# Down products two steps behind the up products in a float32-precise decoder trunk, with every hidden tile turned by DMA and the bias bands loaded in fewer transfers

## The reference

```python
def swiglu(x, w_gate_up, w_down):
    gate, up = jnp.split(x @ w_gate_up, 2, axis=-1)      # 1024 x 5632
    return (jax.nn.silu(gate) * up) @ w_down             # 2816 x 1024

for layer in range(2):
    h = mixer_a(...) if layer == 0 else mixer_b(..., rel_bias)
    x = x + rms_norm(h @ w_o, g[1])
    h = swiglu(rms_norm(x, g[2]), w_gate_up[layer], w_down[layer])
    x = x + rms_norm(h, g[3])

bias = rel_bias[relative_bucket(rel * dilation)]         # a function of the distance, one per head
s = (q @ k) * scale + bias, masked; softmax; @ v
```

## Time and profile before

| | us |
|---|---|
| three runs, median (range) | 759.71 (758.87 to 760.59) |
| profiled execution | 757.09 |
| its span, first to last instruction | 755.3 |
| outside the span | 1.8 |
| PE busy | 744.8 (99%) |
| DVE busy | 531.9 (70%) |
| ACT busy | 416.7 (55%) |
| POOL busy | 175.4 (23%) |

### The profile page before, as it was taken

One profiled execution on the slowest core, in us unless ns is written; L12 is line 12 of the kernel. 1 busy time (PEld: TensorE's weight loads), 2 busy tenths in 40 slices (PEclk: granted clock), 3 DMA queues, 4 the chain that ended last, 5 costly groups with the idle time before them and its releaser, 6 DMA issues.

```text
span 755.3 us, 13376 instructions
## 1 busy us (share of the span) xinstructions
PE 744.8 (99%) x4616; PEld 639.5 (85%) x4616; DVE 531.9 (70%) x766; ACT 416.7 (55%) x619; POOL 175.4 (23%) x298
## 2 busy tenths in 40 slices
PE   9999999999999999999999999999999999999996
PEld 7999987888888888999898898898878888888884
DVE  5888997776766657777777677677557675666653
ACT  4766667444343344865855867766576434433421
POOL 1000001225100000146664664666502000000000
PEclk9999999999999999999999999999999999999999
DMA  8645585699976675559798897897743797767602
GB/s 251 198 126 162 181 245 186 187 275 231 239 250 202 184 223 136 164 157 242 182 219 175 207 190 194 190 223 210 242 140 98 252 277 217 213 192 233 228 14 56
DMA packets 190756, 147.16 MB, mean 195 GB/s; under 512 B 38521, under 2 KB 179425, under 8 KB 190721
## 3 DMA queue, kind: packets, MB, share of 16 engines
q1 hardware_dynamic: 153344, 131.45, 57.0%
q10 hardware_dynamic: 30592, 7.84, 6.4%
q0 software_dynamic: 6784, 7.41, 6.1%
HBM read 138.02 MB, written 1.11 MB: 184 GB/s over the span
## 4 chain that ended last, share of the span: by engine, by line
PE 61%; issue 16%; POOL 10%; DMA 7%; DVE 3%; ACT 1%; POOLq 1%; SPq 0%; DVEq 0%; ACTq 0%
PE ps L1283 16%; PE ps L1284 15%; PE ps L1285 15%; DMA ones<-bias_rows 4%; POOL work L480 4%; POOL work L499 2%; PE ps L1289 2%; PE ps L1291 2%; PE ps L1290 2%; POOL ones L482 2%; DMA work<-work 2%; POOL work L497 2%; DVE w_lo L852 1%; PE ps L1360 1%; PE ps L1377 1%
## 5 line engine op out<-in xcount | busy, mean ns | idle before, releaser
L852 DVE TENSOR_TENSOR w_lo<-raw,w_hi 128x2048 fp32r<-128x2048 f32 (+2 forms) x144 | 279.8, 1961 | 70.7 <-ACT w_hi L542 70.7
L542 ACT ACTIVATE w_hi<-raw 128x2048 fp32r<-128x2048 f32 (+2 forms) x144 | 233.2, 1639 | 99.4 <-DMA raw<-in_w_kv_b 38.0
L1283 PE MATMUL ps<-w_hi,xt 128*128 128x512 f32 x352 | 137.6, 391 | 0.0
L1285 PE MATMUL ps<-w_hi,xt 128*128 128x512 f32 x352 | 137.0, 389 | 0.0
L1284 PE MATMUL ps<-w_lo,xt 128*128 128x512 f32 x352 | 137.0, 389 | 0.0
L716 ACT ACTIVATE work<-ps,stat 128x256 f32<-128x256 f32 x44 | 21.0, 477 | 155.4 <-PE ps L1285 151.2
L449 POOL TENSOR_SCALAR stat<-stat 128x1 f32<-128x1 f32 x15 | 9.6, 639 | 405.8 <-ACT work L558 381.7
L1283 PE MATMUL ps<-w_hi,ot 128*128 128x512 f32 x240 | 95.0, 396 | 0.1
L1284 PE MATMUL ps<-w_lo,ot 128*128 128x512 f32 x240 | 93.6, 390 | 0.0
L1285 PE MATMUL ps<-w_hi,ot 128*128 128x512 f32 x240 | 93.5, 390 | 0.0
L480 POOL DMA_DIRECT2D work<-bias_rows x128 | 74.9, 587 | 43.5 <-DVE ot L1135 26.7
(11 more groups left out here) (157 smaller groups left out, 1274.2 us busy)
## 6 DMA issues: line engine op xcount, KB each, us to landing
raw<-in_w_gate_up SPq DMA_DIRECT2D x88, 512.0 KB, 5.0
raw<-in_w_kv_b SPq DMA_DIRECT2D x96, 256.0 KB, 4.5
raw<-in_w_down SPq DMA_DIRECT2D x22, 1024.0 KB, 5.2
raw<-in_w_q_b SPq DMA_DIRECT2D x48, 256.0 KB, 4.6
raw<-in_w_qkv_a SPq DMA_DIRECT2D x23, 512.0 KB, 5.2
raw<-in_w_o_a SPq DMA_DIRECT2D x4, 1024.0 KB, 6.9
work<-bias_rows POOLq DMA_DIRECT2D x128, 32.0 KB, 3.6
raw<-in_w_o_b SPq DMA_DIRECT2D x4, 1024.0 KB, 5.2
```

What stands on the lines that cost most here:

```text
L542: act.activation(w_hi[:, s % CUT, 0:size(s)], raw[:, s % RAW, 0:size(s)], ACT.Copy).then_inc(hi_made, 1)
L852: dve.tensor_tensor(w_lo[:, c, 0:n], raw[:, s % RAW, 0:n], w_hi[:, c, 0:n].bitcast(F32), ALU.subtract).then_inc(lo_made, 1)
L1283: mm(out, xs[0], ws[0], start=start, stop=False)
L1285: return mm(out, xs[1], ws[0], start=False, stop=stop)
```

## The change

The down products fall one step further behind: PE's order becomes `up(0)`, `up(1)`, `up(2)`, `down(0)`, `up(3)`, `down(1)`, ..., `up(10)`, `down(8)`, `down(9)`, `down(10)`. Units are renumbered to match (down weights are 6, 9, 12, ..., 30, 31, 32). `ot` alternates between two places (`hidden_at`). DVE's order in a step becomes `lo`, `gated(i, 0)`, `lo`, `cut_hidden(i-1)`, `part_planes(i, 0)`, `gated(i, 1)`, `part_planes(i, 1)`, `lo`. The last step is turned by DMA like the others, and `transpose_hidden` goes. SP now holds unit 6, `down(0)`'s weights, behind step 0's transpose. A head's bias rows are loaded once for both tiles, as stretches of 96 words: 8 transfers a head, and the two tiles' additions read them at an offset of 32 words. `own_band` gets its own place, and the wait for `rows_done` goes.

```diff
-                         [[(2 * R - 1) * 2 * RUN, NH], [1, HR], [HR, NT], [2 * RUN, R], [1, RUN]]) for r in range(R)]
+                         [[(2 * R - 1) * 2 * RUN, NH], [1, HR], [2 * RUN, R], [1, SPAN]]) for r in range(R)]
...
             def swiglu(l, s0):                                  # SP
-                gate_up(l, s0, 0, 0)
-                gate_up(l, s0 + 2, 1, 0)
-                two_rows(s0 + 4, 0, down_dram[l][:, 0:2, :])
-                gate_up(l, s0 + 5, 2, 0, behind=planes_at(l, 0))
-                two_rows(s0 + 7, 0, down_dram[l][:, 2:4, :])
+                for i in range(3):
+                    gate_up(l, s0 + up_at(i), i, 0)
+                sp.wait_ge(planes_turned, planes_at(l, 0))
+                two_rows(s0 + 6, 0, down_dram[l][:, 0:2, :])
...
             def head_bias(b, h):                                # POOL
-                    for t in range(NT):
-                        pool.dma_start(band[at_, t].rearrange("p (c n) -> p c n", c=R),
-                                       bands[r][ds(h, 1)][:, :, t].rearrange("h m c n -> (h m) c n")).then_inc(band_in, 16)
-                    pool.dma_start(own_[at_], own_bands[ds(h, 1)].rearrange("h m t n -> (h m) t n")
-                                   ).then_inc(band_in, 16)
-                pool.wait_ge(band_in, (h * 16 + 16) * (R * (NT + 1)))
+                    pool.dma_start(band[at_], bands[r][ds(h, 1)].rearrange("h m c n -> (h m) c n")).then_inc(band_in, 16)
+                    pool.dma_start(own_band[at_], own_bands[ds(h, 1)].rearrange("h m n -> (h m) n")).then_inc(band_in, 16)
+                pool.wait_ge(band_in, (h * 16 + 16) * (2 * R))
...
-            pool.wait_ge(rows_done, 2)
...
             def swiglu_step(l, s0, i, j, units):                # ACT
+                s = s0 + up_at(i)
+                for t, u in enumerate(units[0:NT]):
+                    if i == 1:
+                        silu_of(l, s, i, j, t)
                     hi(u, j)
+                    if i > 1:
+                        silu_of(l, s, i, j, t)
+                planes_ready(l, i, j)
+                if 1 < i < STEPS - 1:
+                    hi(units[NT], j)
+                turn_planes()
+                if i == STEPS - 1 and len(units) > NT:
+                    hi(units[NT])
...
             def swiglu_step(l, s0, i, j, units):                # DVE
                 if i > 1:
                     lo(units[0], j)
+                gated(l, i, j, 0)
+                lo(units[1 if i > 1 else 0], j)
                 cut_hidden(l, i - 1, j, s0)
-                gated(l, i, j, 0)
-                if i < STEPS - 1:
-                    part_planes(l, i, j, 0)
+                part_planes(l, i, j, 0)
                 if i == 1:
-                    lo(units[0])
-                if len(units) > 1:
-                    lo(units[1], j)
+                    lo(units[1])
                 gated(l, i, j, 1)
-                if i < STEPS - 1:
-                    part_planes(l, i, j, 1)
+                part_planes(l, i, j, 1)
                 if len(units) > 2:
                     lo(units[2], j)
...
+                swiglu_step(l, s0, last, 0, [s0 + 3 * last + 1, s0 + 3 * last + 2])
+                if next_unit is not None:
+                    lo(next_unit)
+                cut_hidden(l, last, 0, s0)
...
             def last_steps(l, s0, ahead=None):                  # PE
-                up(l, s, last, 0, 0)
-                up(l, s, last, 0, 1)
-                down_part(l, s + 2, last - 1, 0, 0, FH[:2])
-                transpose_hidden(l)
-                down_part(l, s + 2, last - 1, 0, 0, FH[2:])
+                down_part(l, s + 2, last - 1, 0, 0, FH)
                 down_part(l, s + 2, last - 1, 0, 1, FH[:2])
                 down_part(l, s + 3, last, 0, 0, FH).then_inc(acc_done, 1)
...
             def swiglu_step(l, s0, i, j):                       # PE
+                s = s0 + up_at(i)
                 up(l, s, i, j, 0)
                 up(l, s, i, j, 1)
-                down(l, s + 2, i - 1, j)
+                if i >= 2:
+                    down(l, s + 2, i - 2, j)
```

More of the change, by code:

```diff
@@ L273, in build @@
                              "pt_done", "pt_made", "pvb_done"))
-        up0_done, silu_made, hid_made, ht_done, ht_hi, ht_made = (sem(n) for n in (
-            "up0_done", "silu_made", "hid_made", "ht_done", "ht_hi", "ht_made"))
+        up0_done, silu_made, hid_made, ht_hi, ht_made = (sem(n) for n in (
+            "up0_done", "silu_made", "hid_made", "ht_hi", "ht_made"))
         halves_parted, halves_turned = sem("halves_parted"), sem("halves_turned")
@@ L316, in hidden_at, with up_at @@
         def hidden_at(i):
-            return slice(2, 4) if i == STEPS - 1 else slice(0, 2)
+            first = 2 * (i % 2)
+            return slice(first, first + 2)
+        def up_at(i):
+            return 2 * i if i < 2 else 3 * i - 2
         def by_residue(v):
@@ L377, in pair_b, with gate_up @@
                              q_dram[:, k4, :, cols] if c == 0 else kv_dram[:, c - 1, k4, :, cols])
-            def gate_up(l, s, i, j, behind=None):
+            def gate_up(l, s, i, j):
                 for half in range(2):
-                    if half and behind:
-                        sp.wait_ge(planes_turned, behind)
                     load(s + half, j, lambda r: r.rearrange("p (k c n) -> p k c n", k=4, c=2),
@@ L804, in _ @@
             boundary(0, WOA0 + 3, 2)
-            swiglu(0, FA0, [B0 - 1, B0, B0 + 1])
+            swiglu(0, FA0, range(B0 - 2, B0 + 1))
+            hi(B0 + 1)
             hi(B0 + 2)
@@ L1105, in gated @@
                 dve.wait_ge(silu_made, j * 4 + 2 * n + t + 1)
-                if l and not i:
-                    dve.wait_ge(ht_done, l)
                 dve.scalar_tensor_tensor(hid[:, t, :], bank(4 + t, FC, FC), x_rs(2 * l + 1, t), silu[:, t, :],
@@ L1121, in join_planes, with cut_hidden @@
                 dve.wait_ge(planes_joined, j * 2 + d + 1)
[L1123 removed]
+            def cut_hidden(l, i, j, s0):
                 n, k = l * STEPS + i, hidden_at(i)
                 hi_, lo_ = (ot[:, h, k, :].rearrange("p f (t n) -> p t f n", t=NT) for h in range(2))
[L1126 to L1133 removed]
+                join_planes(l, i, j)
+                if i > 1:
+                    dve.wait_ge(w_used, j * 6 + s0 + 3 * i + 1)
+                dve.tensor_copy(hi_, joined).then_inc(ht_hi, 1)
                 dve.wait_ge(ht_hi, j * 2 + n + 1)
[L1135 removed]
+                dve.tensor_tensor(lo_, joined, hi_.bitcast(F32), ALU.subtract).then_inc(ht_made, 1)
             def swiglu_step(l, s0, i, j, units):
@@ L1231, in _ @@
             boundary(0, FA0 + 2, 2)
-            swiglu(0, FA0, [B0 - 1, B0])
-            cut_hidden(0, STEPS - 1, 0)
+            swiglu(0, FA0, B0)
             for u in range(1, 4):
@@ L1265, in _ @@
             boundary(2, FB0 + 2, 6)
-            swiglu(1, FB0, [UNITS - 1])
-            cut_hidden(1, STEPS - 1, 0)
+            swiglu(1, FB0)
             scale_h(3, 0)
@@ L1438, in up @@
                     inst.then_inc(up0_done, 1)
-            def transpose_hidden(l):
-                pe.wait_ge(hid_made, 2 * (l * STEPS + STEPS))
-                if l:
-                    pe.wait_ge(ht_made, l * STEPS)
-                for f in range(2):
-                    for t in range(NT):
-                        inst = pe.transpose(bank(6, SEQ * f + P * t, P), hid[:, t, P * f:P * f + P], eye[:, :])
-                inst.then_inc(ht_done, 1)
             def down_part(l, s, i, j, t, parts_):
```

69 lines of the change are left out of this document (25 added, 44 removed).

## The result

The changed kernel is slower by about a third of a percent: 761.09 us median (758.69 to 764.68, 22 runs) beside 758.65 (754.59 to 761.97, 22 runs) of the kernel before on the same chip, a ratio of 1.0037 with a 95% interval of 1.0022 to 1.0052. 758.8 had been predicted, with 756.3 to 761.6 as the range: the range holds the time, the direction was wrong. The profiled execution took 760.72 us (757.09 before), with a span of 759.0 (755.3) and a clock of 0.995 (0.998).

The account below looks back on a forecast made before the run. PE, busy nearly throughout, was taken as the bound, with single stalls left to remove. At the median -0.45 - 0.5 - 2.9 + 2.8 + 0.1 = -0.95 us from 759.71 gave 758.8 us, range 756.3 to 761.6.

Parts of the forecast that it names:

- (a): PE's late starts at one down part in each layer go, because `ht_made` has a step more: -0.45 us.
- (b): PE's transposes in both layers' last steps go, 0.90 us, of which layer 0 takes back about 0.4: -0.5 us kept.
- (c): Second attention: fewer band loads end DVE's three waits for POOL, -1.65 us in the profiled execution, -2.9 at the median.
- (d): PE waits in `up(2)` for `gated(1, 1)`, 0.8 us in layer 0 and 2.0 in layer 1: +2.8 us.
- the 3 us that I had named as a sign of being wrong: The forecast counts as wrong if the gap in `up(2)` is missing or above 3 us.
- (e): The last tile's DMA turn, ahead of `down(10)`, costs 0.1 us for both layers' ends, bounds 0 and 1.2.
- (f): Other added work, such as some 2 us of DVE beside `down(8)` and ACT's `hi` and `silu`, stays hidden: no cost.
- three rivals: POOL's lateness worth more, 757.4 us (chance 0.22); costlier feed-forward start, 761.2 (0.20); POOL not freed, 761.7 (0.08).

Follow-up runs that it names:

- bands and early load: Kernel before with the band part and the post gains loaded after the last scores, old feed-forward: 754.72 us, ratio 0.9956.
- the extra load: Changed kernel with one more POOL DMA, head 15's own band loaded again ahead of the wait for `pvb_done`: 755.74 us, ratio 0.9981.
- twelve loads a head: Changed kernel with four one-word loads more per head, 12 in all as before the change: 756.70 us, ratio 0.9979.
- written-out kernel: Changed kernel with POOL's seven loop turns written out, no branch and no registers: 761.27 us, ratio 1.0059.
- padded kernel: Changed kernel with 24 small memsets on POOL behind the loop, ahead of the wait for `pvb_done`: 763.55 us, ratio 1.0089.
- two semaphores: Changed kernel with the own bands counted on a semaphore of their own, same loads in the same order: 760.57 us, ratio 1.0054.

## Why the prediction failed

**(a) Late down parts: right.** PE turns to every down part at 0.227. -0.45 us as forecast, by before's one trace. Two other traces with the old order had more: with the bands alone PE was late by 0.99 and 0.36 us, with bands and early load by 1.65 and 0.49.

**(b) The PE transposes: mis-sized.** I let them go for 0.5 us, because the new `cut_hidden(10)` ends where the old one did and DVE's chain "stays where it is". `cut_hidden` does. But DVE's `lo` of unit B+1 waits for ACT's `hi`, and that now stands behind the turn of the last step, whose `DMA_TRANSPOSE` holds ACT's queue until DVE's planes are made. `hi` started at 294.56, the `lo` behind it at 296.08 (292.34 before), and the load that waits for this `lo` went out at 297.87 (294.12). So DVE's last `lo` and `scale_h` came 2.1 us later than in before, and PE stopped for 1.75 (1.3 to 1.75 in the 14 traces with this order). With `hi` first the gap goes, so this is shown. (b) gives -0.90 + 1.75 = +0.85. The forecast had looked at DVE's order and not at what a moved `hi` holds up two engines further on.

**(c) The bands: the waits went, but that the bands took them is not shown.** All three waits for POOL are gone, and POOL waits for `sum_made`. The second attention without its gap is 2.8 us shorter, where I had 1.65 for the profiled execution and 2.9 at the median. Of the 1.65, one stall was 0.78 us by its starts and not 0.88. Where the two stalls had been the gain is some 1.8; the other 1.0 us had come before any wait for POOL. And the feed-forward part alone, with the old bands and a late 133rd DMA of its own, has no such waits in its trace either, 254.9 us for the second attention (after without its gap: 254.8), and a spread of only 755.48 to 757.21. So old bands don't always make POOL late, what decides it was not tried, and the 2.8 us can't be put down to the bands. How much of it is a gain at all depends on the run: before's 27 runs beside the extra load spread from 754.47 to 760.59, that kernel's 12 from 754.93 to 756.88. The best runs of before are as fast.

**(d) The gaps in `up(2)`: right in place and releaser, too large in this execution.** 0.44 and 0.71 us for 0.8 and 2.0. In layer 1 the step 0 transpose was issued at 585.84 and unit 6 at 589.77, 3.9 us later, where I had taken before's 5.35, and the load landed in 5.07. That `lo` ahead of `gated(1, 1)` is the cause is shown: with `gated` first both gaps are gone. How large they are changes from trace to trace, as the chain says: over the 14 with this order layer 0's was 0.34 to 0.75 us and layer 1's 0.39 to 3.69. With twelve loads a head the turn took 5.7 us and the gap was 2.29; in the written-out kernel the load took 7.6 and the gap was 3.69, past the 3 us that I had named as a sign of being wrong.

**(e) The last turn: right in its result**, no gap at `down(10)`. The two last turns landed in 3.3 and 3.1 us, where I had 4.1 to 5.35, which I had read as turns without and with a load beside them. Both of those had about 0.3 MB of weights moving beside them in before's trace. **(f)** was right but for that `hi`.

**The step that failed is the one I didn't have.** In (c) I counted the 64 fewer DMAs as time that POOL gains. They also move the place of POOL's late 133rd DMA, and for the load of the gains, which in before had gone out at once, the sum had no term at all. Before, the late DMA fell into the middle of head 10, at 452 to 459 us. That the three waits of DVE all come behind it, from 484 us on, fits, but was not tried, and the feed-forward part alone has the same late DMA without the waits. With 8 loads a head it falls on the gains, which DVE needs at once and PE right behind it. The price is 3.71 us of gap and 1.6 at half clock, 5.3 together. The 6.86 us could be read in the trace of before, as the one long gap in POOL's issuing that no wait explains, and I had not asked what they were. None of the three rivals had it either. The time lies close to what two of them gave, 761.2 and 761.7, and inside my range, but that is luck. (d) alone doesn't make it: with the gaps in `up(2)` still there (1.4 us in that trace) and the gains on time the kernel measures 755.74, below before. And POOL was freed.

The sum of the steps as measured: -0.45 + 0.85 - 2.8 + 1.15 + 5.3 = +4.1 us, and PE's last matmul starts 751.78 - 747.57 = 4.2 us later. At the median it is 761.09 - 758.65 = 2.4, since before's profiled execution lay 1.6 us below its median and after's only 0.4.

Neither of the two places in the Trainium skill changed the sum. By the fit in "DMA: Bandwidth & Descriptors", section "Anatomy of one DMA", which is for transfers issued by POOL, unit 6 would land in an estimated 4.4 us, and the trace has 4.89 and 5.07, between the page and my 5.1 to 5.2. Section "Queues, rings and completion order" of the same page has every DMA engine go round its queues packet by packet, so that a turn shares with the loads and doesn't stand behind them. The trace of after agrees in part: 13 turns of hidden tiles beside 0.25 to 0.56 MB of weights reached their last packet in 2.6 to 2.8 us, as did the last one with none, but others took up to 5.2.

## What to carry to other kernels

Fewer DMAs on an engine also mean that each later one has another number. When a trace shows one DMA of a long row late for no visible reason, find out which it is, count, and ask what will stand in that place after the change. A load that an engine needs at once should wait for the earliest event that makes its buffer free and not for the latest one at hand: waiting for `s_done` cost nothing here and took 5.5 us from the span. And when an instruction is moved behind another on a queue, follow the releases that come from it to the load of the next buffer, three units on.

## What the runs showed of the hardware

- One of POOL's DMAs per execution starts late: the 129th from the first band load on, by 3.4 us (3.7 in the padded kernel) where the loads ahead of it had landed, by 4.2 to 6.9 in the middle of a head, there 1.80 us after the last landing. A load of one word can take the lateness upon itself.
- At every gap of 3.5 to 5.3 us between two matmuls (11 in 10 traces) the granted clock fell to half (1.2 GHz), from 2.4 us before PE's next matmul to 1.4 after it, and stayed there for 3.41 us, or for 6.83 (padded kernel, gap of 5.27 us; two semaphores, 3.84 us). At gaps of 1.3 to 2.3 us it did not.
- The turn of a hidden tile took 2.6 us from issue to the last packet with no weight load under way (the last of layer 1, before and after). Beside loads it took 2.6 to 5.2 in after and 3.5 to 8.4 in before.
